# Interleaving the modulation megabytes with their step's panel, and folding layer 0's norm weight and offset into the column factors

## The reference, cut to what matters

```python
c_act = silu(c)
for l in range(2):
    shift, scale, gate = split(c_act @ w_mod[l] + b_mod[l], 3)
    h = x * (1 + scale) + shift
    y = attention(h)              # differential (l = 0), forgetting (l = 1)
    x = layer_norm(alpha * x + gate * y, ln_g[l], ln_b[l])
```

## Time and profile before

| | us |
|---|---|
| median of 3 runs | 2741.72 |
| their range | 2737.67 to 2751.97 |
| the profiled execution's own time | 2757.5 |
| its span | 2755.6 |
| PE busy | 2501.9 (91%) |
| DVE busy | 1714.8 (62%) |
| ACT busy | 1041.8 (38%) |
| moved by DMA | 699.74 MB, mean 254 GB/s |

### The profile page before, as it was taken

The page is one execution under the profiler, slowest core; times in us unless marked ns, Lnnn a source line. Parts: engine busy times, 40 slices in busy tenths (PEclk is TensorE's granted clock), DMA queues, the critical chain, the costliest instruction groups (busy, mean ns, idle before and its releaser), DMA issues.

```text
span 2755.6 us, 42740 instructions
## 1 busy us (share of the span) xinstructions
PE 2501.9 (91%) x18111; PEld 2059.6 (75%) x18111; DVE 1714.8 (62%) x2630; ACT 1041.8 (38%) x1556; POOL 177.4 (6%) x289
## 2 busy tenths in 40 slices
PE   5799999798789799989998958899899999999998
PEld 1588877566656598789854848578699898998986
DVE  4657789688767755356524755777755477655555
ACT  0253343344453333344423322344444444343443
POOL 1102233011100000111000000000000000000000
PEclk7799999899899899989977975999999999999999
DMA  9969999787678688969766748868645587755553
GB/s 353 337 219 356 349 336 313 234 294 288 244 260 308 244 286 308 353 209 312 258 220 218 249 90 309 327 232 276 236 133 189 183 274 276 244 184 191 188 171 107
DMA packets 317373, 699.74 MB, mean 254 GB/s; under 512 B 13600, under 2 KB 14080, under 8 KB 312192
## 3 DMA queue, kind: packets, MB, share of 16 engines
q1 hardware_dynamic: 298432, 627.27, 66.2%
q0 software_dynamic: 18480, 67.66, 7.0%
q10 hardware_dynamic: 272, 2.10, 0.2%
HBM read 646.77 MB, written 56.49 MB: 255 GB/s over the span
## 4 chain that ended last, share of the span: by engine, by line
PE 73%; DVE 15%; DMA 8%; ACT 2%; issue 1%; SPq 0%; POOL 0%; DVEq 0%; ACTq 0%; POOLq 0%
PE bank L2147 71%; DVE arena L1352 5%; DMA ring<-in_w_mod 3%; DMA ring<-in_a_w_in 3%; DVE ring_lo L1352 3%; DVE sm L1352 2%; DVE arena L1360 2%; PE bank L2150 1%; PE bank L2375 1%; DMA ring<-in_a_w_out 1%; DMA arena<-arena 0%; DVE MSB L1352 0%; DMA m_state<-MSB 0%; DVE LT L1360 0%; ACT att_w_hi L963 0%
## 5 line engine op out<-in xcount | busy, mean ns | idle before, releaser
L1352 DVE TENSOR_TENSOR ring_lo<-ring,w_hi 128x1024 fp32r<-128x1024 f32 (+1 forms) x380 | 427.7, 1134 | 359.9 <-ACT w_hi L963 334.8
L963 ACT CAST w_hi<-ring 128x1024 fp32r<-128x1024 f32 x316 | 330.6, 1049 | 472.5 <-PE bank L2147 470.4
L1352 DVE TENSOR_TENSOR ring_lo<-ring,att_w_hi 128x1024 fp32r<-128x1024 f32 x192 | 232.0, 1223 | 224.1 <-ACT att_w_hi L963 223.9
L963 ACT CAST att_w_hi<-ring 128x1024 fp32r<-128x1024 f32 x192 | 198.9, 1049 | 350.8 <-PE bank L2147 181.0
L2147 PE MATMUL bank<-in_hi,w_hi 128*128 128x256 f32 x1024 | 290.2, 283 | 1.2 <-DVE n L1357 1.2
L2147 PE MATMUL bank<-in_lo,w_hi 128*128 128x256 f32 x1024 | 290.1, 283 | 0.0
L2147 PE MATMUL bank<-in_hi,ring_lo 128*128 128x256 f32 x1024 | 289.7, 283 | 0.0
L2147 PE MATMUL bank<-w_hi,hid_lo 128*128 128x512 f32 x640 | 257.5, 402 | 5.2 <-DVE ring_lo L1352 5.2
L2147 PE MATMUL bank<-ring,cpad 128*32 128x512 f32 x1408 | 195.7, 691 | 26.1 <-DMA ring<-in_w_mod 22.5
L2147 PE MATMUL bank<-att_w_hi,att_hi 128*128 128x512 f32 x512 | 206.0, 402 | 6.9 <-DVE ring_lo L1352 6.9
L2147 PE MATMUL bank<-ring_lo,att_hi 128*128 128x512 f32 x512 | 202.7, 396 | 0.0
(11 more groups left out here) (259 smaller groups left out, 4998.5 us busy)
## 6 DMA issues: line engine op xcount, KB each, us to landing
ring<-in_w_mod SPq DMA_DIRECT2D x192, 1024.0 KB, 9.5
ring<-in_a_w_in SPq DMA_DIRECT2D x64, 1024.0 KB, 10.2
ring<-in_w_mlp_in SPq DMA_DIRECT2D x64, 1024.0 KB, 5.2
ring<-in_w_mlp_out SPq DMA_DIRECT2D x64, 1024.0 KB, 5.1
ring<-in_kv_w_mod SPq DMA_DIRECT2D x32, 1024.0 KB, 10.7
ring<-in_b_w_in SPq DMA_DIRECT2D x32, 1024.0 KB, 6.9
ring<-in_kv_w SPq DMA_DIRECT2D x32, 1024.0 KB, 5.6
ring<-in_s_w_glu SPq DMA_DIRECT2D x32, 1024.0 KB, 5.5
```

What stands on the lines that cost most here:

```text
L963: a.copy(whi(h), raw_half(h)).then_inc(*o.up("whi"))
L1352: return v.tensor_tensor(dst, x, y, op).then_inc(*(to or o.up("dve")))
```

## The change

- Blocks 23 to 25 leave the attention loop. Blocks 23 to 26 go to steps 0 to 3, 27 and 28 between steps 3 and 4, and 29 to 36 to steps 4 to 11. Block 37 goes from PE to DVE (steps 12 and 13), and DVE's blocks 38, 39, 40 move two steps later each; the last four pieces of block 40 are done in iterations 0 to 3 of the second attention's loop. The blocks of that loop start at `t` = 5 instead of 2.
- In the steps of `MOD_AT_STEP` the ring's order is now one chunk of the panel, one chunk of the block, and so on. PE multiplies the block's chunk after every second half, and issues `sums` of the former block at the start of `multiply(n)`. ACT's code for these blocks stays behind `round_of(n)`.
- `layer_norm(0)` makes only `xhat`, with one `tensor_scalar` (128 x 2048) for each token tile. The factor of the transposed `q` columns becomes `(1 + scale) * ln_g` and the offset `(1 + scale) * ln_b + shift`; `ln_g` and `ln_b` are loaded as columns for it (two more small row copies at the start). The full `x` is made in 16 `ln_piece` operations (128 x 512) in steps 4 and 5; the transposes for `k` and the store of `x` wait for it.
- The load of `p3` is issued after the waits for `ms0` and `ms1`.

```diff
-MOD_AT_A = {5: 23, 9: 24, 13: 25}
-MOD_AT_STEP = {0: 26, 1: 27, 2: 28, **{n: 26 + n for n in range(4, 12)}}
-MOD_AT_LN = (29,)
-MOD_AT_B = {2 + 5 * i: 41 + i for i in range(6)}
+MOD_AT_STEP = {**{n: 23 + n for n in range(4)}, **{n: 25 + n for n in range(4, 12)}}
+MOD_AT_LN = (27, 28)
+MOD_AT_B = {5 + 5 * i: 41 + i for i in range(6)}
-DVE_MOD = {38: 12, 39: 14, 40: 16, 47: 20, 48: 24, ...
+DVE_MOD = {37: 12, 38: 14, 39: 16, 40: 18, 47: 20, 48: 24, ...
-SUMS_AT = {12: 37, 14: 38, 16: 39, 18: 40, 20: 46, ...
+SUMS_AT = {12: 36, 14: 37, 16: 38, 18: 39, 20: 46, ...
+DVE_PART[N_W1 - 1, 3] = DVE_PART.pop((N_W1, 0))
...
@@ sync_program
                     load(key, W, k0, n0, q)
+                    if key[0] == "step" and key[1] in MOD_AT_STEP:
+                        j = MOD_AT_STEP[key[1]]
+                        load(("mod", j), MOD_W[MODS[j][0]], 0, 128 * MODS[j][1], q)
...
             sp.wait_ge(S["blm"], 32)
-            sp.dma_start(reg(4096, 4096), proj_d[3]).then_inc(S["p3"], 16)
             sp.wait_ge(S["ms0"], 16 * 16)
             sp.wait_ge(S["ms1"], 16 * 16)
-            for t in sorted(MOD_AT_A):
-                mod(MOD_AT_A[t])
+            sp.dma_start(reg(4096, 4096), proj_d[3]).then_inc(S["p3"], 16)
...
@@ vector_program
+                    if n in (N_Q, N_Q + 1):
+                        ln_piece(8 * (n - N_Q) + h - 8 * n - 4)
...
+            def ln_piece(i):
+                t2, c = i // 8, i // 2 % 4
+                cs = slice(512 * c, 512 * c + 512)
...
+                if i % 2 == 0:
+                    tt(xv[:, t2, cs], xv[:, t2, cs], lnG0[c], MUL)
+                else:
+                    tt(xv[:, t2, cs], xv[:, t2, cs], lnB[:, cs], ADD, *o.up("ln" if c == 3 else "dve"))
...
+                if l == 0:
+                    own()
+                    for t2 in range(2):
+                        ts(xv[:, t2, :], xv[:, t2, :], mv[:, t2, 0:1], st[:, 6 + t2:7 + t2], SUB, MUL, *o.up("xhat"))
+                    return
...
-                if n == N_Q - 1:
-                    mod_bias("m1s")
                 if n == N_Q:
                     layer_norm(0)
-                    own()
-                    ts(sc1, M("m1", 16), 1.0, None, ADD, None, *o.up("scol"))
-                    split_in("q", h_raw["q"], sc1, M("m1", 0), AHk, ALk, N_Q, 8 * n)
+                    mod_bias("m1s")
+                    own()
+                    stt(sc1, M("m1", 16), 1.0, C("lng"), ADD, MUL)
+                    stt(q_shift, M("m1", 16), 1.0, C("lnb"), ADD, MUL)
+                    own()
+                    tt(q_shift, q_shift, M("m1", 0), ADD, *o.up("scol"))
+                    split_in("q", h_raw["q"], sc1, q_shift, AHk, ALk, N_Q, 8 * n)
...
+                if t < 4:
+                    mod_piece(N_W1 - 1, 4 + t)
...
@@ tensor_program
+            def mod_part(j, q):
+                w = chunk("mod", j, q)
+                p.wait_ge(*landed("mod", j, q))
+                if q == 0:
+                    room("mod", j)
+                for i in range(4):
+                    t = mm(bank("mod", j)[32 * i:32 * i + 32, :], cwide[:, 4 * q + i, :], w[:, i, :], q == 0, q == 3)
+                t.then_inc(*(fill("mod", j) if q == 3 else (S["taken"], 1)))
...
             def multiply(n):
+                if n in MOD_AT_STEP and MOD_AT_STEP[n] - 1 not in SUMS_AT.values():
+                    sums(MOD_AT_STEP[n] - 1)
...
+                    if r % 2 and n in MOD_AT_STEP:
+                        mod_part(MOD_AT_STEP[n], r // 2)
...
-                    p.wait_ge(S["ln"], 2)
+                    p.wait_ge(S["xhat"], 2)
                     turn_in("q", xv)
                 elif n == N_K:
+                    p.wait_ge(S["ln"], 2)
                     turn_in("k", xv)
...
                 multiply(n)
                 if n in SUMS_AT:
                     sums(SUMS_AT[n])
-                if n in MOD_AT_STEP:
-                    mod(MOD_AT_STEP[n])
```

More of the change, by code:

```diff
@@ L135, in step @@
             ring.use(("step", n, q), slots)
+            if n in MOD_AT_STEP:
+                ring.use(("mod", MOD_AT_STEP[n], q), slots)
         for b in range(2):
             bank.use(("step", n, b), GD)
+        if n in MOD_AT_STEP:
+            bank.use(("mod", MOD_AT_STEP[n]), GM)
     def tile(i):
@@ L260, in build @@
                  "gq", "gx", "gs", "gz", "oth", "hhi", "hlo", "whi", "wlo", "gated", "gsq", "relu2", "hidhi", "hid",
-                 "pcol", "xn", "xres", "xsq", "ysq", "ones", "dtaken", "dmod"]
+                 "pcol", "xn", "xres", "xsq", "ysq", "xhat", "ones", "dtaken", "dmod"]
         S = {n: ctx.enter_context(nc.semaphore(n)) for n in names}
@@ L396, in mod_acc @@
         def mod_acc(j):
-            at = MSB if j > 47 else L2
-            return at[:, 512 * (DVE_NO[j] % 2):512 * (DVE_NO[j] % 2) + 512]
+            i = DVE_NO[j] % 2
+            return MSB[:, 512 * i:512 * i + 512] if j > 47 else (L2[:, 0:512], L1[:, 1536:2048])[i]
         def mod_base(j):
@@ L488, in build @@
         bcA, lnG, lnB = reg(24576, 2048), reg(26624, 2048), MSB[:, :]
+        lnG0 = [L2[:, 512 * i:512 * i + 512] for i in range(3)] + [L1[:, 1536:2048]]
+        q_shift = st[:, 176:192]
         res_tmp = sm[:, 0:512]
@@ L2183, in mod @@
                 for q in range(4):
-                    w = chunk("mod", j, q)
-                    p.wait_ge(*landed("mod", j, q))
-                    if q == 0:
-                        room("mod", j)
-                    for i in range(4):
-                        t = mm(bank("mod", j)[32 * i:32 * i + 32, :], cwide[:, 4 * q + i, :], w[:, i, :], q == 0, q == 3)
-                    t.then_inc(*(fill("mod", j) if q == 3 else (S["taken"], 1)))
+                    mod_part(j, q)
+            def mod_part(j, q):
[6 more added lines that the diff above has]
+                t.then_inc(*(fill("mod", j) if q == 3 else (S["taken"], 1)))
             def turn_scaled():
```

34 lines of the change are left out of this document (16 added, 18 removed).

## The result

The changed kernel takes 2773.95 us (median of 4 runs, 2771.68 to 2776.53), the kernel before 2742.39 us (4 runs, 2737.67 to 2751.97): ratio 1.0111, 95% interval 1.0082 to 1.0140. The prediction was 2749.5 us with a range up to 2768, so it missed by 24.5 us, on the slow side. The profiled execution has a span of 2769.9 us.

The account below looks back on a forecast made before the run. The prediction took PE, busy 91% of the span, as the bound, so PE work added in busy stretches costs its full length. Its terms summed to +7.8 us on the 2741.72 us median: 2749.5 us, range 2727 to 2768.

Parts of the forecast that it names:

- the wait at the boundary: At step starts, PE's sums wait for ACT's copy of the former block: 0.75 or 1.3 us each.
- Steps 0 to 3: One more block less a quarter +3.6, seam idle won -4.0, boundary waits +2.3, shape changes +4.8: +6.7 us.
- Steps 4 to 11: Added block work +3.6, seven boundary waits +9.1, shape changes +9.6, store of `x` and late ring +1.5: +23.8 us.
- Start and `m_state`: Up to the attention loop: extra row copies +1.0 us; last `m_state` write lands sooner without `p3` beside it, -5.5 us.
- Attention loop: DVE's three long waits for PE at the modulation blocks go with the blocks: -12.3 us.
- Change of shape: PE switching between full and 128x32 matmuls four times a block instead of once: +1.2 us a block.
- Layer norm: Two `tensor_scalar` replace eight DVE operations, but PE has two blocks between and waits for weights: -1.3 us.
- Step 11 to 12: DVE makes `scol` for `k` sooner, as its chunk's slot frees a quarter step earlier: -7.0 us.
- Second attention's loop: `sums(40)` enters the loop, 1.4 us, and four DVE pieces lie around the first scores, 1.0: +2.4 us.
- late chunks: Rival: chunks land late, moving ACT and PE back 1.5 to 2.5 us at ten boundaries; some 2769 us, chance 0.27.
- Cheap seams: Rival: shape turns 0.3 a block, ACT's copy 0.5 a boundary, block 28's weights in time; 2730 us, chance 0.18.
- The norm's gain is not there: Rival: layer norm gives 0 and DVE's pieces delay steps 4 and 5 by 3 us: 2754 us, no separate chance.

Follow-up runs that it names:

- second profile: The kernel before, unchanged, run and profiled once more on this chip: span 2738.9 us, median 2740.7 us.
- e3: Kernel before with only the load of `p3` moved behind the waits for `m_state`: 2749.3 us, ratio 1.0017 to the kernel before.
- e5: e1 with each block's four parts multiplied in two pairs, in the ring's order too: 2740.0 us, ratio 0.9977 to the kernel before.
- e10: Kernel before with only the norm's weight and offset moved into column factors and full `x` made in pieces: 2741.2 us, ratio 0.9979.
- e2: Changed kernel with each step's block loaded and multiplied whole behind its step, kv bias one step later: 2746.1 us, ratio 1.0007 to the kernel before.
- e12: e8 with four unread one-column matmuls behind each deliberate wait: 2764.0 us, ratio 1.0071 to the kernel before.
- e6: e1 with blocks mixed into steps 3 and 11 only, behind the step in the other ten: 2749.4 us, ratio 1.0015 to the kernel before.
- e7: e1 with 16 unread one-column matmuls where PE idles ahead of the second S5 layer: 2740.3 us, ratio 0.9985 to the kernel before.
- e1: Changed kernel with the former block's sums moved from the step's start to behind its third half: 2743.9 us, ratio 0.9993 to the kernel before.
- e9: e1 with block parts in pairs in every step but 3, and 16 unread matmuls: 2731.1 us, ratio 0.9944 to the kernel before.
- e8: e1 with graded deliberate waits of 0.74 to 2.22 us on GpSimd memsets at step boundaries: 2752.3 us, ratio 1.0019 to the kernel before.
- e11: Changed kernel with its boundary wait kept and only the sums moved behind the step's third half: 2760.0 us, ratio 1.0061 to the kernel before.
- e4: e1 with deliberate waits for GpSimd memsets at boundaries, some 5.0 us long: 2758.7 us, ratio 1.0059 to the kernel before.
- e13: e1 with four unread one-column matmuls at the start of steps 5 to 11, no wait: 2746.5 us, ratio 1.0018 to the kernel before.

## Why the prediction was wrong

It fell at one step above all, **the wait at the boundary** in "Steps 0 to 3" and "Steps 4 to 11". Its mechanism and its length were right: seven waits of 1.3, 9.1 us, against 9.5 measured. Its price was taken as its length. With the sums right behind it, it also brought the granted clock down, for 11.0 us more of busy PE in steps 4 to 11. The text names a lower clock there among what would make it wrong, and gives it no rival and no price. A row for one was there: the layer norm, where PE is idle most, has a clock of 0.72, and steps 4 to 11, where it never is, 0.99.

Against the second profile the sum is 23.3 us short: 9.3 in steps 4 to 11, 5.9 in steps 0 to 3, 5.1 in the second attention's loop and 5.9 in the tail, less 2.9 elsewhere. Point by point:

- *Start and `m_state`*: -4.7 for -4.5. Right by luck. The write gained 1.8 us here and 3.4 in the median of all profiles, not 5.5. The other 2.9 us is when that write was issued (729.9 against 732.8), which lies between 727.5 and 736.9 over all profiles whatever the kernel. The +1.0 is borne out: the first weight chunk is issued 0.8 us later.
- *Attention loop*: -14.2 for -12.3 (-12.6 against the first profile, whose three waits the term was read from; in the second these are 7.66, 3.13 and 3.13, in all 13.9). Right. That the gain stays only when the blocks leave the loop too, e3 shows.
- *Steps 0 to 3*: +12.6 for +6.7 (+8.7 against the first profile). The waits were 2.02, 0.70 and 0.70 for three of 0.75; the first is near the prediction's own bound for a chunk that lands late. The 4.0 us to be won at the seams were mostly one execution's: the second profile has 0.75 us of idle time there. Its 2.88 us in step 0, the largest part of the 6.9, the sum doesn't mention, and every run kept it. The clock took about 3 us of busy time: it loses 6.1 here, 2.5 in the first profile and 1.5 in the second, and of the 6.1 only 1.7 stands behind sums (ahead of step 1); 3.4 stands around the wait in step 0.
- *Change of shape*: 0.92 to 1.1 a block for 1.2. Right, inside its bounds. e5 shows that it isn't all shape.
- *Layer norm*: -1.9 for -1.3. The net is right, by two terms that e10 pulls apart: -7.8 for the fold, and nearly 6 back for the second block, 2.5 of it waits for its weights. The working had both: transposes at T + 14.0, measured T + 14.6.
- *Steps 4 to 11*: +33.1 for +23.8. The sum without clock would have been 226.7 + 9.5 = 236.2, less than the 238.5 of the prediction, whose +1.5 for the store shows in e2 and e10 (1.3) and not in the mixed kernels.
- *Step 11 to 12*: -7.6 for -7.0. Right.
- *Second attention's loop*: +7.5 for +2.4 against the second profile, -1.4 against the first. Nine of the runs on the change's base have 125.1 to 125.7 us, the changed kernel 129.6, e12 129.4, e6 133.5; with DVE's pieces as before it is 122.1 and 131.0, 122.2 in e3 and 125.1 in e10. The length follows what the clock loses in the loop: 18.8 us in the second profile and e3, 22.2 in e10, 23.9 in each of the nine, 29.0 in the changed kernel and e12, 30.7 in the first profile, 34.1 in e6. Whether a part of it is the change's stays open.
- *The tail*: +5.9 for 0, the largest error after the clock. Block 37 was costed at nothing for PE because a wait covered it; its 16 matmuls were also 16 places in the stream (e7). Not all of it is that: the clock loses 65.6 us there in the changed kernel, 60.9 in the second profile and 62.8 in e7.

Of the rivals, *late chunks* gave the right sign and nearly the size, 2769, by a mechanism that can explain one boundary (2.02 us), not ten; the 2.31 us has a load of the activation table in it, 1.28 us, ahead of the first sigmoid. *Cheap seams* was wrong: no seam was cheap. *The norm's gain is not there* was wrong too: the gain is there, -1.9. With the sums where nothing waits for them the change is worth nothing that can be measured (e1, 0.9993), and with fewer turns and its old place in the stream 0.56% (e9).

## What to carry to other kernels

Price a new short wait on PE together with what PE does right behind it: a wait of 1.1 us was free of clock with full matmuls behind it and cost, at most boundaries, another 1.7 us with four one-column matmuls there. Put small matmuls that need a fresh copy into the middle of dense work, half a step after the copy can be there, and look at the granted clock in windows before and behind each seam. When a change adds or drops instructions early in PE's stream, compare the "issue" waits of unchanged stages further on before explaining their time by the change.

## What the runs showed of the hardware that was not expected

- Waits of PE of 0.74 to 2.72 us alone left its clock at 1.00 in steps 4 to 11 (e8 and e11, seven of seven boundaries each). The 2.88 us in step 0 lost 1.7 or 3.4 us in twelve of sixteen profiles, one of 3.41 us ahead of step 1 lost 1.7 (e11), and waits of 5.0 us lost 1.3 to 2.0 us (e4).
- A wait of 1.00 to 2.31 us followed by 0.95 us of one-column matmuls lost 1.7 or 3.4 us at three of five boundaries (e12) and six of seven (steps 4 to 11 of the changed kernel); waits of 0.63 us with them lost none (two of two, e12), nor did the columns alone (seven of seven, e13).
- Sixteen matmuls more in the stream took 4 to 5 us of "issue" waits out of stages that hadn't changed (e7 against e1, one profile each).
